# High and low parts of the values as one TensorE operand in an attention layer, with the halves added on GpSimd

## What is computed

```python
def reference(x, p, ...):
    h = x
    u = rmsnorm(h, mix_norm_g[0])
    h = h + sliding_window_attention(u, a_wqkv[0], ..., a_wo[0])
    h = h + sqrelu_mlp(rmsnorm(h, mlp_norm_g[0]), m_w1[0], m_w2[0])
    gate = jax.nn.sigmoid(rmsnorm(h, ple_norm_g[0]) @ ple_w_gate[0])
    return h + gate * (p[0] @ ple_w_proj[0])

def sliding_window_attention(u, wqkv, gq, gk, sinks, wo):   # core of it
    scores = jnp.einsum('bnqkgd,bnskd->bnkgqs', qb, kb) * (HD ** -0.5)
    scores = scores - slopes * dist                          # ALiBi, then the mask
    m = jnp.maximum(scores.max(axis=-1), sink)
    e = jnp.exp(scores - m[..., None])
    probs = e / (e.sum(axis=-1) + jnp.exp(sink - m))[..., None]
    o = jnp.einsum('bnkgqs,bnskd->bnqkgd', probs, vb)
    return o.reshape(b, s, H * HD) @ wo
```

## Time and profile before

| | us |
|---|---|
| median of 3 runs | 1079.7 (1078.48 to 1079.87) |
| the profiled execution | 1078.62 |
| its span in the profile | 1076.9 |
| PE busy | 1059.7 (98% of the span) |
| VectorE busy | 783.7 (73%) |
| ScalarE busy | 471.9 (44%) |
| GpSimd busy | 169.2 (16%) |

### The profile page before, as it was taken

The page is one execution under the profiler, slowest core; times in us unless marked ns, Lnnn a source line. Parts: engine busy times, 40 slices in busy tenths (PEclk is TensorE's granted clock), DMA queues, the critical chain, the costliest instruction groups (busy, mean ns, idle before and its releaser), DMA issues.

```text
span 1076.9 us, 14194 instructions
## 1 busy us (share of the span) xinstructions
PE 1059.7 (98%) x4936; PEld 876.6 (81%) x4936; DVE 783.7 (73%) x1127; ACT 471.9 (44%) x819; POOL 169.2 (16%) x277
## 2 busy tenths in 40 slices
PE   7899999999999999999999999999999999999998
PEld 5778888887888888888888888888888888888887
DVE  6877777788344599776677668476776878747985
ACT  6566666677323233412322342353333334437451
POOL 8665555553000000000000000000000000001000
PEclk9999999999999999999999999999999999999999
DMA  8101110050332325353343244998998898760102
GB/s 313 46 34 40 40 40 21 37 196 20 118 117 79 117 71 205 135 195 117 144 188 140 92 188 187 372 412 286 285 290 291 290 321 302 254 234 1 40 30 88
DMA packets 67468, 171.74 MB, mean 159 GB/s; under 512 B 5200, under 2 KB 5456, under 8 KB 67280
## 3 DMA queue, kind: packets, MB, share of 16 engines
q1 hardware_dynamic: 67408, 170.95, 44.4%
HBM read 133.18 MB, written 37.75 MB: 159 GB/s over the span
## 4 chain that ended last, share of the span: by engine, by line
PE 88%; DVE 5%; POOL 3%; issue 2%; ACT 2%; ACTq 0%; POOLq 0%; DVEq 0%
PE pair L2530 28%; PE pair L2510 22%; PE pair L2256 9%; PE pair L2393 8%; PE pair L2576 7%; PE pair L2322 3%; PE pair L2468 3%; PE pair L2290 2%; PE pair L2605 2%; PE pair L2301 1%; PE pair L2438 1%; POOL bias L840 1%; ACT probs L1048 1%; PE pair L2275 1%; PE pair L2235 0%
## 5 line engine op out<-in xcount | busy, mean ns | idle before, releaser
L2530 PE MATMUL pair<-uT 128*128 128x512 f32 x1344 | 305.9, 389 | 0.0
L2530 PEld LDWEIGHTS pair<-uT 128*128 128x128 f32 x1344 | 252.0, 188 | 52.5 <-DVE uT L1959 0.4
L1304 ACT ACTIVATE uT<-wo_raw 128x1024 fp32r<-128x1024 f32 x83 | 84.8, 1054 | 114.1 <-PE pair L2530 97.2
L1959 DVE TENSOR_TENSOR uT<-wo_raw,uT 128x1024 fp32r<-128x1024 f32 x83 | 98.6, 1222 | 46.1 <-ACT uT L1304 45.6
L785 POOL TENSOR_SCALAR row_var<-row_ssq 128x1 f32<-128x1 f32 x16 | 4.0, 250 | 706.4 <-ACT hn L1345 623.2
L2393 PE MATMUL pair<-WA,oT 128*128 128x512 f32 x384 | 90.3, 392 | 0.5 <-DVE oT L1719 0.3
L2393 PEld LDWEIGHTS pair<-WA,oT 128*128 128x128 f32 x384 | 71.2, 188 | 15.8 <-issue 1.3
L2510 PE MATMUL pair<-WA,WB 128*128 128x512 f32 x336 | 78.2, 389 | 0.4 <-ACT xr L1279 0.4
L2510 PEld LDWEIGHTS pair<-WA,WB 128*128 128x128 f32 x336 | 63.0, 188 | 13.8 <-DVE WB L1893 0.8
L2576 PE MATMUL pair<-WA 128*128 128x512 f32 x288 | 68.1, 391 | 0.0
L2576 PEld LDWEIGHTS pair<-WA 128*128 128x128 f32 x288 | 53.7, 188 | 11.0
(11 more groups left out here) (242 smaller groups left out, 1884.9 us busy)
## 6 DMA issues: line engine op xcount, KB each, us to landing
wo_raw<-in_m_w SPq DMA_DIRECT2D x71, 512.0 KB, 6.7
wo_raw<-hid_kept SPq DMA_DIRECT2D x41, 512.0 KB, 6.2
hid_kept<-RES SPq DMA_DIRECT2D x32, 512.0 KB, 2.7
emb<-in_m_w SPq DMA_DIRECT2D x17, 512.0 KB, 6.2
RES<-in_m_w SPq DMA_DIRECT2D x8, 1024.0 KB, 6.7
uT_f<-in_m_w SPq DMA_DIRECT2D x6, 1024.0 KB, 6.9
RES<-in_a_wqkv SPq DMA_DIRECT2D x10, 512.0 KB, 8.3
emb<-hid_kept SPq DMA_DIRECT2D x10, 512.0 KB, 6.1
```

The lines of the kernel that those rows point to most:

```text
L1304: nc.scalar.activation(operand(t, which, HI), unit(t, which), ACT.Copy).then_inc(op_hi, 1)
L1959: nc.vector.tensor_tensor(operand(t, which, LO), unit(t, which), operand(t, which, HI).bitcast(F32), ALU.subtract).then_inc(op_ready, 1)
L2530: mm = nc.tensor.matmul(ps[4 * (j % 2) + m][:], operand(t, 0, s)[:, k, m * P:(m + 1) * P], operand(t, 1, r)[:, k, :], start=(g == 0 and k ...
```

## The change

The array `vz` is laid out so that the high and the low part of one head lie side by side, 128 columns. One matmul then gives the product with the high part in rows 0 to 63 of the bank and that with the low part in rows 64 to 127. Four matmuls a step replace six (and the product LO with LO is now part of it). `attention_out` copies both halves out: two activations more a step, into `ring`, one row for even and one for odd blocks. GpSimd adds the low half to `RES` in `add_low`, two instructions of 128x512 a block, placed a block later; for the last block they stand at the end of the stage. The semaphore `current_ready` becomes `current_then_lows`, which counts these additions too; `attention_out` and `oT_hi_half` wait on it. Since the ring is now in use up to the end of the stage, SP loads the first two w1 pieces only after the last addition, and the first `xr` before them. GpSimd's loop takes two blocks a turn.

```diff
-        vz = sb("vz", [P, 2, 2, KV * HD], F32R, in_a)
+        vz = sb("vz", [P, 2, KV, 2, HD], F32R, in_a)
...
+        def low_out(par, at, cols):
+            return ring[:, par, at:at + cols]
+        def lows(n):
+            return 2 + 2 * n
+        def by_head(v):
+            return v[:].rearrange("p (v d) -> p v d", d=HD)
...
             for k in range(4):
                 if k >= 2:
                     sp.wait_ge(w_split, U_W1 + k - 1)
-                else:
-                    sp.wait_ge(w_split, U_W1)
+                elif k == 0:
+                    sp.wait_ge(biased, H * NB)
+                    sp.dma_start(xr[:], x[0:P, :]).then_inc(xr_in, 16)
+                    sp.wait_ge(current_then_lows, lows(NB))
                 sp.dma_start(ring[:, k % 2, :].rearrange("p (k n) -> p k n", k=2),
                              rows_of(w1, k, 0, BANK)).then_inc(ring_in[k % 2], 16)
                 if k == 1:
-                    sp.wait_ge(biased, H * NB)
-                    sp.dma_start(xr[:], x[0:P, :]).then_inc(xr_in, 16)
                     load_residual(1)
...
-                copy(vz[:, 0, HI, :], vprev[:]).then_inc(dv_moved, 1)
+                copy(vz[:, 0, :, HI, :], by_head(vprev)).then_inc(dv_moved, 1)
...
+            def add_low(n, par, hf):
+                stand(pool, attended, 4 * n + 2 * hf + 2)
+                o = RES[:].rearrange("p b n -> p (b n)")[:, bass.ds(n * D + hf * BANK, BANK)]
+                pool.tensor_tensor(o, o, low_out(par, hf * BANK, BANK), ALU.add).then_inc(current_then_lows, 1)
...
                 dv_hi_part(n)
+                add_low(n - 1, 1 - par, 0)
                 mask_probs(4 * n)
...
                     place_sinks(n + 1, 0)
+                add_low(n - 1, 1 - par, 1)
                 mask_probs(4 * n + 2)
...
             mask_probs(NB * GROUPS - 1)
+            add_low(NB - 1, 1, 0)
+            add_low(NB - 1, 1, 1)
...
-            def attention_out(n, j):
+            def attention_out(n, j, par):
...
-                mine = slice(HD * (j % 2), HD * (j % 2 + 1))
+                if j % 2 == 0 and not (isinstance(n, int) and n < 2):
+                    act.wait_ge(current_then_lows, lows(n - 2) + j // 2 + 1)
                 flat = RES[:].rearrange("p b n -> p (b n)")
                 for odd in range(2):
-                    moved = nc.scalar.activation(flat[odd * HD:(odd + 1) * HD, bass.ds(n * D + j * 2 * P, 2 * P)],
-                                                 pv_bank[mine, odd * 2 * P:(odd + 1) * 2 * P], ACT.Copy)
+                    rows = slice(odd * HD, (odd + 1) * HD)
+                    nc.scalar.activation(flat[rows, bass.ds(n * D + j * 2 * P, 2 * P)],
+                                         pv_bank[0:HD, odd * 2 * P:(odd + 1) * 2 * P], ACT.Copy)
+                    moved = nc.scalar.activation(low_out(par, j * 2 * P, 2 * P)[rows],
+                                                 pv_bank[HD:P, odd * 2 * P:(odd + 1) * 2 * P], ACT.Copy)
                 moved.then_inc(attended, 1)
...
-                    act.wait_ge(attended, GROUPS * (b + 1))
+                    act.wait_ge(current_then_lows, lows(b + 1))
...
-                    act.wait_ge(attended, NB * GROUPS)
+                    act.wait_ge(current_then_lows, lows(NB))
...
-                nc.vector.tensor_tensor(vz[:, 1, LO, :], vnext[:], vz[:, 1, HI, :].bitcast(F32),
+                nc.vector.tensor_tensor(vz[:, 1, :, LO, :], by_head(vnext), vz[:, 1, :, HI, :].bitcast(F32),
...
-                    for s, m in PASSES:
-                        at = 2 * HD * (j // 2)
-                        mm = nc.tensor.matmul(pv_bank[:], vz[:, kt, s, at:at + 2 * HD], pT[:, m, kt, :],
-                                              start=(done == 0), stop=(done == 5))
+                    for m in (HI, LO):
+                        mm = nc.tensor.matmul(pv_bank[:], vz[:, kt, j, :, :].rearrange("p s d -> p (s d)"), pT[:, m, kt, :],
+                                              start=(done == 0), stop=(done == 3))
```

More of the change, by code:

```diff
@@ L405, in trunk_layer @@
         dist_step = sem("dist_step")
-        current_ready = sem("current_ready")
+        current_then_lows = sem("current_then_lows")
         bias_first = sem("bias_first")
@@ L812, in _ @@
             pool.memset(vprev[:], 0.0).then_inc(zeros_ready, 1)
-            pool.memset(current[:], 1.0).then_inc(current_ready, 1)
-            pool.wait_ge(current_ready, 1)
+            pool.memset(current[:], 1.0).then_inc(current_then_lows, 1)
+            pool.wait_ge(current_then_lows, 1)
             pool.affine_select(out=current[:], in_=current[:], compare_op=ALU.is_ge, fill=0.0,
-                               base=0, pattern=[[-1, P]], channel_multiplier=1).then_inc(current_ready, 1)
+                               base=0, pattern=[[-1, P]], channel_multiplier=1).then_inc(current_then_lows, 1)
             pool.iota(dist[:], pattern=[[-1, 2 * P]], base=P, channel_multiplier=1,
@@ L886, in place_sinks, with body @@
                                    ALU.mult).then_inc(sink_placed, 1)
-            def body(n, last=False):
+            def body(n, par, last=False):
                 head_norm("q8", n)
@@ L938, in _ @@
             place_sinks(1, 0)
[L939 to L942, removed]
+            body(1, 1)
+            with pool.Fori(0, (NB - 4) // 2) as m:
+                body(2 * m + 2, 0)
+                body(2 * m + 3, 1)
+            body(NB - 2, 0)
+            body(NB - 1, 1, last=True)
             mask_probs(NB * GROUPS - 1)
+            add_low(NB - 1, 1, 0)
+            add_low(NB - 1, 1, 1)
             with pool.Fori(0, NB) as b:
@@ L1021, in v_hi_part @@
                 wait(act, pv_done, 4 * b)
-                nc.scalar.activation(vz[:, 1, HI, :], vnext[:], ACT.Copy).then_inc(v_hi, 1)
+                nc.scalar.activation(vz[:, 1, :, HI, :], by_head(vnext), ACT.Copy).then_inc(v_hi, 1)
             def k_hi_part(b, par):
@@ L1081, in last_part @@
                     pT_hi_part(t - 1, (j - 1) % 2)
-                    attention_out(n - 1, 2)
+                    attention_out(n - 1, 2, 0)
                     q_hi_part("q8", n, 0)
@@ L1090, in last_part @@
                 pT_hi_part(t - 1, (j - 1) % 2)
-                attention_out(*before(n, j, 2))
+                attention_out(*before(n, j, 2), 1 if j >= 2 else 0)
                 if j == 1:
@@ L1129, in body @@
                     if not (first and j < 2):
-                        attention_out(*before(n, j, 2))
+                        attention_out(*before(n, j, 2), par if j >= 2 else 1 - par)
                     if j == 0:
@@ L1187, in _ @@
             body(NB - 1, 1, last=True)
-            attention_out(NB - 1, GROUPS - 2)
+            attention_out(NB - 1, GROUPS - 2, 1)
             pT_hi_part(NB * GROUPS - 1, 1)
@@ L1191, in _ @@
             oT_hi_half(2, 0)
-            attention_out(NB - 1, GROUPS - 1)
+            attention_out(NB - 1, GROUPS - 1, 1)
             oT_hi_half(2, 1)
@@ L1581, in v_lo_part @@
                 dve.wait_ge(v_hi, b + 1)
-                nc.vector.tensor_tensor(vz[:, 1, LO, :], vnext[:], vz[:, 1, HI, :].bitcast(F32),
+                nc.vector.tensor_tensor(vz[:, 1, :, LO, :], by_head(vnext), vz[:, 1, :, HI, :].bitcast(F32),
                                         ALU.subtract).then_inc(v_ready, 1)
                 dve.wait_ge(dv_moved, 2 * b + 1)
-                nc.vector.tensor_tensor(vz[:, 0, LO, :], vprev[:], vz[:, 0, HI, :].bitcast(F32),
+                nc.vector.tensor_tensor(vz[:, 0, :, LO, :], by_head(vprev), vz[:, 0, :, HI, :].bitcast(F32),
                                         ALU.subtract).then_inc(v_ready, 1)
@@ L1591, in add_bias @@
                 if first:
-                    dve.wait_ge(current_ready, 2)
+                    dve.wait_ge(current_then_lows, 2)
                 for half_bank in range(2):
```

## The result

The changed kernel takes 1088.5 us (median of 4 runs, 1087.8 to 1090.3) against 1079.1 us (4 runs): the ratio is 1.009, 95% interval 1.0072 to 1.0107. The forecast was 1082.8 us with a range up to 1086.0. The direction was right, the size was not: +9.4 us in place of +3.1. The profiled execution took 1087.8 us with a span of 1086.0 us.

What follows compares the result with a forecast made beforehand. PE's stretch and a chain through ScalarE, VectorE and GpSimd were taken to bound each block. Six blocks at 0.70 − 0.46 gave +1.4, block 7 +1.7: +3.1 us on the 1079.7 median, 1082.8 us, range 1076.5 to 1086.

Steps and rivals of the forecast that it cites:

- The structure: Attention blocks: two stretches in a row, PE's own 11.0 us, then 18.3 us through ScalarE, VectorE and GpSimd.
- −2.8 us for the six blocks: Blocks 1 to 6: only the j = 0 `weigh_values` lies in PE's stretch, saving 0.46 us in each block.
- Rival 3: PE bounds everything and all 64 removed matmuls come off, 14.8 us: 1064.9 us; chance 0.06.
- rival 1: GpSimd's addition lets VectorE through or VectorE is first; delay 0.36 us a block, about 1080.3 us; chance 0.28.
- Rival 2: The chain has unseen slack (`v_hi_part` not awaited, or extra copies hide), so PE's stretch gains 2.8 us: 1076.9 us; chance 0.12.
- I cost it at nothing: Second `add_low`, behind `shift_k`: VectorE's next instruction with two SBUF inputs starts over a microsecond later, so no cost.
- the price that the prediction gave for lost cover: Second `add_low`: 0.5 us a block if VectorE's next instruction with two SBUF inputs did not come late enough.
- First addition and copies, 0.70 us a block: Blocks 1 to 6: ScalarE's extra copies and the first `add_low` lengthen the chain by 0.36 to 0.85 us a block.
- the bounds of −0.6 to +2.3: Blocks 1 to 6 together, in us: chain delay of 0.36 or 0.85 a block less 0.46 saved; +1.4 taken.
- Block 7, +1.7 us: Block 7: extra copies delay `v_hi_part` and the later `exps`, partly taken up elsewhere; bounds +0.8 to +2.5 us.
- Behind the stage, 0: After attention: w1 loads land at 286 us, but PE needs `oT_hi_half` only near 292.5, so no cost.
- Rival 4: The w1 loads come late enough to stop PE, 1 to 3 us on top: about 1085 us; chance 0.06.

Runs made afterwards that it cites:

- the four matmuls alone: Changed kernel without the copies of the low half and with both additions one column wide: 1073.95 us, ratio 0.9953 to the kernel before.
- v_hi first everywhere: Changed kernel with the second addition behind the masks in blocks 1 to 5 and `v_hi_part` ahead of `attention_out` in every block: 1080.45 us.

## Why the prediction was wrong in size

- **The structure was right, but not in block 6.** A block is PE's stretch and then a chain over the other engines; some three fifths of what PE saves it spends waiting. PE had 14.8 us less to do and the four matmuls alone gave 5.9. The forecast's −2.8 us for the six blocks measured −5.4 (177.85 to 172.43), by block 0.81, 0.73, 0.73, 0.74, 0.74 and 1.67 us. In block 3 `turn_q` of q8 comes 0.46 us sooner behind the block's `scores`, just as forecast; but `v_hi_part` comes 0.61 sooner, the squares of k 0.72 and the next `scores` 0.73, so the second stretch gains another 0.27, on ScalarE. And block 6 of the kernel before, 30.64 us long, doesn't end in a wait. Its `scores` (7,0) follow `turn_probs` without idle time:

```profile
237.04 0.60 PE L2301 MATMUL pair<-ident,probs 128*128 128x128 f32 x4
237.40 1.20 PE L2290 MATMUL pair<-kT,qT 128*128 128x256 f32 x8
```

  There nearly all of the four `weigh_values` comes off (4 × 0.46 = 1.8 us). The prediction counted block 6 as one like the others. Rival 3 (1064.9) is out, and so is rival 1, as `scale_probs` is held up in five of six blocks. Rival 2 had it that VectorE doesn't wait for `v_hi_part`; with `v_hi_part` sooner even the kernel before is 1.2 us shorter in the six blocks.
- **The step that failed: "I cost it at nothing".** The second `add_low` was given the cover that VectorE's next instruction with both inputs in SBUF, behind `k_lo_part`, comes more than a microsecond later. That passed over `nmax` at the end of `add_bias`: 128x4, 0.16 us, ahead of `k_lo_part`. It was not priced, though the earlier trace rows name it as what ScalarE's `exps` wait for. It waits 1.17 us in four blocks, 4.7 us; moving the addition shortens the six blocks by 4.6. Even the price that the prediction gave for lost cover, 0.5 us a block, was too low: it is 0.78 on the mean of six blocks and 1.17 where it strikes.
- **First addition and copies, 0.70 us a block.** Both mechanisms are there: `scale_probs` at 1.47 us, v_hi late by 0.76. They cost 177.70 − 172.43 = 5.3 us in six blocks, 0.9 each, a little above the upper bound of 0.85. Set against what the matmuls gave, blocks 1 to 5 without the second addition's stall are 0.12 us longer on the mean (forecast 0.24), and block 6 is 0.77 shorter, in all −0.15 us: inside the bounds of −0.6 to +2.3 but not at +1.4. Two terms were off in opposite directions, and that this part stayed inside the bounds is luck. One working in it doesn't come out either: the mask's 0.88 less its delay behind L1582 (135.28 to 135.67) is 0.49 us, not 0.64; that 0.64 is right all the same is what other masks show (0.63 to 0.66).
- **Block 7, +1.7 us.** It measured +3.8. The half clock that came with PE's waits was not in the sum: 2.3 us. The rest, 1.5, is near 1.7, and with v_hi first and full clock 1.2 is left (37.04 and 37.07 in two versions). But the sum had the copies alone in it, and the additions have a price of their own. Without the copies, at full clock in the profiled run, block 7 is 1.2 us longer than with the matmuls alone (36.88 against 35.71), and a `scale_probs` near the stage's end is held up by the addition (0.69 us elsewhere):

```profile
263.61 1.70 DVE L1651 TENSOR_TENSOR probs<-probs,rden 128x512 f32<-128x512 f32 x1
...
263.46 1.29 POOL L896 TENSOR_TENSOR RES<-RES,ring 128x512 f32<-128x512 f32 x1
```

  With the copies and small additions it is 4.35 us longer, of which the half clock is 2.8 (2.05 and 4.93 us for 1.17 and 2.98). So either alone is worth 1.2 to 1.5 us and both 1.7; that the sum's size fits is in part luck.
- **Behind the stage, 0.** Right: 0.3 us. Rival 4 did not come.
- Of the 6.3 us by which the forecast missed, 4.7 are the second addition and 2.1 block 7; the other terms together come to −0.5.

What stays open: why the clock falls in some runs and not in others with the same waits (below), and why ScalarE gains the 0.27 us a block; the trace says only where (0.15 at `v_hi_part`, 0.12 at the squares of k).

## What to carry to other kernels

When an instruction is put on GpSimd, list every VectorE instruction with two SBUF inputs that can start while it runs, the tiny ones too: a 0.16 us instruction on the chain pays the whole length of the GpSimd one. A cover has to be checked at each copy of the loop body, the unrolled last ones above all, since the same move that gained 4.5 us in the loop lost 3.0 in block 7. And where two delays meet at one instruction, take each out alone and both together before either is called cheap: here moving v_hi gave 0.8 us in the six blocks, moving the first addition 2.5, and both 5.0. Where a stretch can fall to half clock, compare the stretches ahead of it and not only the whole time: one forecast here was hit because a clock fall made up for a wrong term.

## What was not expected of the hardware

- **The clock in block 7.** With the same instructions in block 7 and the same two waits of PE (1.80 and 0.72 us), the granted clock fell in one version and not in another. The first windows are of the version with the second addition moved and v_hi first in block 7 alone, the second of the one with v_hi first everywhere:

```profile
252.00:255.00 3.00, 2.95 (x8) 2.32 (x9) 2.97 (x5) 2.53 (x9) 0.65 (x1) 0.55 0.00 0
```

```profile
251.00:254.00 3.00, 2.73 (x11) 2.01 (x12) 2.97 (x5) 2.67 (x10) 0.65 (x1) 1.00 0.00 0
```

  Twelve matmuls of `project_out` took 3.88 us in the first and 2.98 in the second. In the run without low copies four executions of one kernel split in two: 1084.4 and 1085.0 us at a mean clock of 0.998, 1087.3 and 1087.9 us at 0.995 and 0.994. The profiled one of them is that of 1084.4 us, and its block 7 is at full clock. That the others lost their 3 us there isn't shown, as no trace of them was kept; but between versions whose block 7 has the same instructions the table has differences of 1.1 and 1.3 us (39.69 and 38.63, 38.33 and 37.04), as much as several single edits here are worth.
- **The addition's price.** 1.29 us for 128x512 on GpSimd with both inputs in SBUF, 1.27 to 1.30 in 14 of 16 cases, and 1.63 and 1.74 in the two where VectorE has started first. Half of L801's 1.90 us (128x1024) was too low a start for the estimate. The Trainium skill ("GPSIMD Engine Reference", section 3.1, on elementwise cycle accounting) has about 2.6 cycles an element for this operation, at 1.2 GHz; by that an estimate is 1.11 us, and the row is 0.18 us above it.
